# Softplus of the prompt attention by a capped exponent: the minimum on VectorE in place of the absolute value on ScalarE

## The chip, the cores and the metric

The kernel runs on one core of a Trainium2 chip. The metric is the device time in microseconds of one execution, the median of several; three runs of the kernel before gave 1794.58, 1794.62 and 1795.06.

## What is computed

One step of a hybrid decoder layer: a projection, stick-breaking attention and gated linear attention in parallel head groups, an output projection, an MLP and a final norm, for a prompt of 1024 tokens and for 8 sequences of 8 new tokens. What the change touches is the stick-breaking attention of the prompt (8 heads of 64, scores `z` with a bias, causal):

```python
log_stay = jnp.where(causal, jax.nn.log_sigmoid(-z), 0.0)
log_after = lax.cumsum(log_stay, axis=3, reverse=True) - log_stay
w = jnp.where(causal, jnp.exp(jax.nn.log_sigmoid(z) + log_after), 0.0)
return jnp.einsum("bhqk,bkhd->bqhd", w.astype(v.dtype), v)
```

Since log_sigmoid(-z) = -softplus(z) and log_sigmoid(z) = z - softplus(z), a weight is exp(z minus the sum of softplus over this key and all later ones). The kernel computes softplus, takes the sums off the scores by a matmul with a triangle of -1, and exponentiates.

## The kernel before

The stage is `stage_prompt_attention` (from line 1290). It stands between the sample attention and the gated linear attention and is closed by a barrier of all engines. Four pairs of heads are worked one after the other. A pair has twelve units, one for each block of 128 keys and chunk of 512 queries (`BLOCKS`): keys 7 down to 0 against the second chunk, then 3 down to 0 against the first. Blocks on the diagonal are narrower. With both heads together, the twelve units of a pair have 256, 512, 768 and five times 1024 columns, then 256, 512, 768 and 1024. This makes 48 units, called u below; `z(u, h)` is a unit's scores in two PSUM banks, out of a ring of three such slots (`NZ`).

Each engine has its own loop over steps s with a fixed order, and they meet by semaphores:

- TensorE (loop behind `subtract_later`, `carry`, `multiply`): scores of unit s (waits for the weights of s - 3, which frees the slot), the sums of unit s - 2 taken off its scores (waits for the low part of its softplus, and for the carry), the carry sum of s - 2, and the product with the values of unit s - 3.
- ScalarE: `absolute(s)`, `weights(s - 2)` (exponential out of PSUM, waits for the sums), `carry_hi(s - 2)`, then `exp_and_log(s)`, which is exp(-|z|) and log(1 + that), both within `pa_a`.
- VectorE: for the last unit of a chunk the two output instructions of unit s - 4 (`output`), then `softplus(s - 1)`: max(z, 0) + log (L1503, waits for the logarithm), the copy to the high part `pa_sh` (L1508), the low part `pa_sl` by subtraction (L1510); then `carry_lo(s - 2)` (L1518), which the next unit's sums wait for.
- SyncE loads queries and keys of a pair two pairs ahead, GpSimd scales the queries; both have nothing else to do here.

The lines which the argument names: L1464 absolute value, L1469 exponential, L1472 logarithm, L1478 weights, L1485 high carry (ScalarE); L1503, L1508, L1510, L1518, L1525 and L1527 (outputs) on VectorE; L1391 to L1400 scores, L1409 to L1415 sums, L1426 and L1428 carries, L1442 values on TensorE. L1918 lies in the stage behind.

Of the kernel before, what the change touches and what calls it, by code (L numbers as in the profile page):

```python
# [16 lines left out]
ALU = mybir.AluOpType  # L17
ACT = mybir.ActivationFunctionType
# [38 lines left out]
class Program:  # L57
# [22 lines left out]
    def sb(self, name, shape, dt=F32, ctx=None):  # L80
        return (ctx or self.ctx).enter_context(self.nc.sbuf_tensor(name, shape, dt))
# [27 lines left out]
def at_least(eng, sem, value):  # L109

    if not isinstance(value, int) or value > 0:
        eng.wait_ge(sem, value)
# [1177 lines left out]
def stage_prompt_attention(g, ops):  # L1290
# [9 lines left out]
    NPAIR = HEADS // 2  # L1300
    TOTAL = NPAIR * NB
    NZ, NA, NS, NW = 3, 3, 3, 3
    HALF = slice(0, HD), slice(HD, P)

    def block_of(u):
        c, j = BLOCKS[u % NB]
        return u // NB, c, j

    def left(c, j):
        return max(0, j - c * QB) * P  # L1310

    def width(u):
        p, c, j = block_of(u)
        return 512 - left(c, j)

    def halves(u):
        return [slice(0, 2)]

    def first(u):
        return u % NB in (0, 8)  # L1320

    def last(u):
        return u % NB in (7, 11)

    def carries_before(u):
        return NCARRY * (u // NB) + CARRY[u % NB]

    def multiplied(u):
        return u + 1

    with ExitStack() as ctx:
        sb = lambda *a: g.sb(*a, ctx=ctx)
        a_ = sb("pa_a", [P, NA, 2, 512])
# [2 lines left out]
        w = sb("pa_w", [P, NW, 2, 512])  # L1336
        later = ops.later
        s_z = g.sem("pa_scored")
        s_abs = g.sem("pa_abs")
        s_exp = g.sem("pa_exp")  # L1340
        s_ln = g.sem("pa_ln")
        s_sp = g.sem("pa_softplus")
        s_sh = g.sem("pa_softplus_hi")
        s_sl = g.sem("pa_softplus_lo")
# [12 lines left out]
        def z(u, h):  # L1357
            n = 2 * (u % NZ)
            return Z[:, n + h.start:n + h.stop, 0:width(u)]

        def ring(t, depth, u, h):
            return t[:, u % depth, h, 0:width(u)]

        with g.nc.Block() as block:
            @block.sync
            def _(sp):
                ops.load(sp, 0, 0)
                ops.load_values(sp)
                ops.load(sp, 1, 1)
                for p in range(2, NPAIR):  # L1370
                    sp.wait_ge(s_z, 2 * NB * (p - 1))
                    ops.load(sp, p, p % 2)
# [8 lines left out]
            def _(pe):  # L1381
                def score(u):
# [7 lines left out]
                    for h in range(2):  # L1390
                        pe.matmul(g.bank[2 * (u % NZ) + h][:, 0:n], ops.k[p % 2][HALF[h], keys], ops.q[p % 2][HALF[h], cols],  # L1391
                                  start=True, stop=False)
                    for h in range(2):
                        done = pe.matmul(g.bank[2 * (u % NZ) + h][:, 0:n], ops.bias[HALF[h], 2 * p + h, :], ops.ones[HALF[h], 0:n],
                                         start=False, stop=not diagonal)
# [36 lines left out]
                def multiply(u):  # L1432
# [7 lines left out]
                    for h in range(2):  # L1440
                        head = (2 * p + h) * HD
                        done = pe.matmul(O[HALF[h], x:512], ops.v[:, j, head:head + HD], w[:, u % NW, h, 0:n], start=first(u),  # L1442
                                         stop=last(u), skip_group_check=True)
# [12 lines left out]

            @block.scalar
            def _(act):
                def absolute(u):
                    for h in halves(u):  # L1460
                        n = 2 * u + h.stop
                        at_least(act, s_sl, n - 2 * NA)
                        act.wait_ge(s_z, n)
                        act.activation(ring(a_, NA, u, h), z(u, h), ACT.Abs).then_inc(s_abs, h.stop - h.start)  # L1464

                def exp_and_log(u):
                    for h in halves(u):
                        act.wait_ge(s_abs, 2 * u + h.stop)
                        act.activation(ring(a_, NA, u, h), ring(a_, NA, u, h), ACT.Exp, scale=-1.0).then_inc(s_exp, h.stop - h.start)  # L1469
                    for h in halves(u):  # L1470
                        act.wait_ge(s_exp, 2 * u + h.stop)
                        act.activation(ring(a_, NA, u, h), ring(a_, NA, u, h), ACT.Ln, bias=1.0).then_inc(s_ln, h.stop - h.start)  # L1472

                def weights(u):
                    at_least(act, s_pv, multiplied(u - NW))
                    for h in halves(u):
                        act.wait_ge(s_y, 2 * u + h.stop)
                        act.activation(ring(w, NW, u, h), z(u, h), ACT.Exp).then_inc(s_w, h.stop - h.start)  # L1478

                def carry_hi(u):  # L1480
                    if last(u):
                        return
                    m, x = carries_before(u), left(*block_of(u)[1:])
                    act.wait_ge(s_cs, m + 1)
                    act.copy(later[m % 2][:, x:512], C[:, x:512]).then_inc(s_eh, 1)  # L1485

                for s in range(TOTAL + 2):
                    if s < TOTAL:
                        absolute(s)
                    if s >= 2:  # L1490
                        weights(s - 2)
                        carry_hi(s - 2)
                    if s < TOTAL:
                        exp_and_log(s)

            @block.vector
            def _(dve):
                def softplus(u, h):
                    n = 2 * u + h.stop
                    inc = h.stop - h.start  # L1500
                    a = ring(a_, NA, u, h)
                    dve.wait_ge(s_ln, n)
                    dve.scalar_tensor_tensor(out=a, in0=z(u, h), scalar=0.0, in1=a, op0=ALU.max, op1=ALU.add).then_inc(s_sp, inc)  # L1503
                    dve.wait_ge(s_sp, n)
                    at_least(dve, s_y, n - 2 * NS)
                    if u >= NS:
                        dve.wait_ge(s_cs, carries_before(u - NS + 1))
                    dve.tensor_copy(ring(sh, NS, u, h), a).then_inc(s_sh, inc)  # L1508
                    dve.wait_ge(s_sh, n)
                    dve.tensor_tensor(ring(sl, NS, u, h), a, ring(sh, NS, u, h), ALU.subtract).then_inc(s_sl, inc)  # L1510

                def carry_lo(u):
                    if last(u):
                        return
                    m, x = carries_before(u), left(*block_of(u)[1:])
                    rows = HALF[1]
                    dve.wait_ge(s_eh, m + 1)
                    dve.tensor_tensor(later[m % 2][rows, x:512], C[rows, x:512], later[m % 2][rows, x:512],  # L1518
                                      ALU.subtract).then_inc(s_e, 1)

                def output(u):
                    p, c, j = block_of(u)
                    cols = slice(c * 512, (c + 1) * 512)
                    dve.wait_ge(s_pv, multiplied(u))
                    dve.tensor_copy(g.op_hi[:, p, cols], O).then_inc(s_oh, 1)  # L1525
                    dve.wait_ge(s_oh, 2 * p + 2 - c)
                    dve.tensor_tensor(g.op_lo[:, p, cols], O, g.op_hi[:, p, cols], ALU.subtract).then_inc(s_ol, 1)  # L1527

                ops.bias_rows(dve)
                samples = g.sample_o[:].rearrange("d p s q -> d p (s q)")  # L1530
                dve.tensor_copy(g.op_hi[:, 0:4, TP:T], samples).then_inc(s_so, 1)
                dve.wait_ge(s_so, 1)
                dve.tensor_tensor(g.op_lo[:, 0:4, TP:T], samples, g.op_hi[:, 0:4, TP:T], ALU.subtract).then_inc(s_so, 1)
                dve.wait_ge(s_so, 2)
                for s in range(TOTAL + 4):
                    if s >= 4 and last(s - 4):
                        output(s - 4)
                    parts = halves(s - 1) if 0 <= s - 1 < TOTAL else []
                    if parts:
                        softplus(s - 1, parts[0])  # L1540
                    if 0 <= s - 2 < TOTAL:
                        carry_lo(s - 2)
                    for h in parts[1:]:
                        softplus(s - 1, h)


def stage_gla(g):
# [9 lines left out]
    QS = GK ** -0.5  # L1557
    HALF = slice(0, GK), slice(GK, P)
    with ExitStack() as ctx:
# [103 lines left out]
        with nc.Block() as block:  # L1663
            @block.sync
            def _(sp):
# [29 lines left out]
                for h in range(2):  # L1695
                    for m in range(2):
                        sp.dma_start(s0[HALF[h], :, 2 * m + h, :], s0d[h, m]).then_inc(s_s0, 16)
                weights(6)
# [1123 lines left out]
```

## Time and profile before

| | before |
|---|---|
| median of 3 runs | 1794.62 us |
| profiled execution | 1795.72 us |
| its span | 1794.1 us |
| TensorE busy | 1657.8 us (92%) |
| VectorE busy | 724.1 us (40%) |
| ScalarE busy | 594.3 us (33%) |
| GpSimd busy | 432.5 us (24%) |

The profile is one execution. The page cuts its span into 40 equal slices of 44.9 us. A view by windows gives busy time in a stretch; the timeline has single instructions with start and length, and in brackets how long the engine stood idle ahead of one and what ended that. A busy engine is not one at its peak: matmuls overlap, and their ends are modelled.

### The profile page before, as it was taken

How to read it: one execution, taken by the hardware profiler on the slowest of the kernel's cores; microseconds unless marked ns; L12 is line 12 of the kernel's file. 1: busy time of each engine (PE TensorE's matmuls, PEld its weight loads, DVE VectorE, ACT ScalarE, POOL GpSimd, SP SyncE). 2: the span in 40 equal slices, each digit the busy share in tenths (PEclk: the TensorE clock that was granted, in tenths of full speed). 3: DMA queues.
4: the chain of work that ended last, by engine and by line, in shares of the span. 5: the costliest groups of instructions: out<-in, count | busy, mean ns of one | idle time of the engine just before them, and what ended most of it. 6: DMA issues, size and time to landing. Idle time of an engine off the chain costs nothing. (4 is left out here: it accounts for less than half of the span.)

```text
span 1794.1 us, 27592 instructions
## 1 busy us (share of the span) xinstructions
PE 1657.8 (92%) x10864; PEld 1449.6 (81%) x10864; DVE 724.1 (40%) x1157; ACT 594.3 (33%) x1010; POOL 432.5 (24%) x305
## 2 busy tenths in 40 slices
PE   5899997999979998587599899999999999999997
PEld 2898996777755554366499799999999999999997
DVE  2511021454457777478214733232323232323225
ACT  3521121333248887345235421202021212121123
POOL 0122112222200000201245542413242323323230
PEclk7899998999989999677699899999999999999999
DMA  9123126666420000853623211011111111111102
GB/s 335 48 98 106 53 100 205 222 186 220 136 107 24 24 1 1 274 176 123 220 94 110 79 48 42 29 47 47 47 47 47 47 47 30 40 46 47 47 12 100
DMA packets 116400, 166.62 MB, mean 93 GB/s; under 512 B 6970, under 2 KB 80141, under 8 KB 116054
## 3 DMA queue, kind: packets, MB, share of 16 engines
q1 hardware_dynamic: 111088, 148.58, 25.2%
q0 software_dynamic: 5120, 16.78, 2.9%
q8 instruction: 59, 0.97, 0.2%
q14 instruction: 31, 0.25, 0.0%
q10 hardware_dynamic: 102, 0.03, 0.0%
HBM read 143.03 MB, written 22.35 MB: 92 GB/s over the span
## 5 line engine op out<-in xcount | busy, mean ns | idle before, releaser
L469 PE MATMUL psum<-op_hi,out_hi 128*128 128x384 f32 (+1 forms) x960 | 320.9, 334 | 3.6 <-DVEq L2617 1.9
L471 PE MATMUL psum<-op_hi,out_lo 128*128 128x384 f32 (+1 forms) x960 | 314.6, 328 | 0.0
L470 PE MATMUL psum<-op_lo,out_hi 128*128 128x384 f32 (+1 forms) x960 | 314.5, 328 | 0.0
L469 PE MATMUL psum<-mlp_a_hi,out_hi 128*128 128x384 f32 (+1 forms) x768 | 251.0, 327 | 0.5 <-DVE x1T L2644 0.5
L471 PE MATMUL psum<-mlp_a_hi,out_lo 128*128 128x384 f32 (+1 forms) x768 | 250.8, 327 | 0.0
L470 PE MATMUL psum<-mlp_a_lo,out_hi 128*128 128x384 f32 (+1 forms) x768 | 250.5, 326 | 0.0
L2534 POOL TENSOR_TENSOR out_lo<-out_raw,out_hi 128x2048 fp32r<-128x2048 f32 x31 | 143.2, 4620 | 271.7 <-ACT out_hi L2557 271.7
L2630 DVE TENSOR_TENSOR mlp_sq<-mlp_relu 128x384 f32<-128x384 f32 (+1 forms) x96 | 88.3, 921 | 280.0 <-ACT mlp_relu L2572 280.0
L469 PEld LDWEIGHTS psum<-op_hi,out_hi 128*128 128x128 f32 x960 | 181.7, 189 | 7.8 <-DVEq L2617 2.8
L470 PEld LDWEIGHTS psum<-op_lo,out_hi 128*128 128x128 f32 x960 | 181.6, 189 | 2.5
L471 PEld LDWEIGHTS psum<-op_hi,out_lo 128*128 128x128 f32 x960 | 181.5, 189 | 0.0
L2644 DVE SCALAR_TENSOR_TENSOR x1T<-psum,modT,x1T 128x384 f32<-128x384 f32 (+1 forms) x192 | 108.6, 570 | 162.1 <-PE psum L471 155.1
L2557 ACT CAST out_hi<-out_raw 128x2048 fp32r<-128x2048 f32 x31 | 59.1, 1908 | 295.9 <-PE psum L471 295.9
L469 PEld LDWEIGHTS psum<-mlp_a_hi,out_hi 128*128 128x128 f32 x768 | 144.2, 188 | 0.8 <-POOL out_lo L2534 0.8
L471 PEld LDWEIGHTS psum<-mlp_a_hi,out_lo 128*128 128x128 f32 x768 | 144.2, 188 | 0.0
L470 PEld LDWEIGHTS psum<-mlp_a_lo,out_hi 128*128 128x128 f32 x768 | 144.1, 188 | 0.0
L2541 POOL TENSOR_TENSOR mlp_a_lo<-mlp_sq,mlp_a_hi 128x384 fp32r<-128x384 f32 (+1 forms) x96 | 92.7, 973 | 207.6 <-ACT mlp_a_hi L2564 207.6
L2572 ACT ACTIVATE mlp_relu<-psum 128x384 f32<-128x384 f32 (+1 forms) x96 | 45.5, 474 | 266.1 <-PE psum L471 266.1
L469 PE MATMUL psum<-op_hi,pg_hi 128*128 128x384 f32 (+1 forms) x192 | 76.4, 398 | 12.8 <-DVE pg_lo L1202 11.5
L590 POOL TENSOR_TENSOR in_lo<-in_raw,in_hi 128x2048 fp32r<-128x2048 f32 (+1 forms) x8 | 34.7, 4334 | 196.4 <-ACT in_hi L724 196.4
L469 PE MATMUL psum<-in_hi,op_hi 128*128 128x256 f32 (+1 forms) x288 | 81.4, 282 | 0.0
L471 PE MATMUL psum<-in_hi,op_lo 128*128 128x256 f32 (+1 forms) x288 | 80.4, 279 | 0.0
(339 smaller groups left out, 2988.5 us busy)
## 6 DMA issues: line engine op xcount, KB each, us to landing
sa_k<-in_cache_k SPq DMA_DIRECT2D x64, 256.0 KB, 3.0
sa_v<-in_cache_v POOLq DMA_DIRECT2D x64, 256.0 KB, 3.9
out_raw<-in_w_up SPq DMA_DIRECT2D x16, 1024.0 KB, 5.4
out_raw<-in_w_down SPq DMA_DIRECT2D x16, 1024.0 KB, 4.9
ada_w<-in_w_ada SPq DMA_DIRECT2D x26, 512.0 KB, 5.0
out_raw<-in_w_out SPq DMA_DIRECT2D x12, 1024.0 KB, 4.8
in_raw<-in_w_in SPq DMA_DIRECT2D x8, 1024.0 KB, 6.0
ada_w<-in_w_ada SPq DMA_DIRECT2D x3, 2048.0 KB, 13.7
```

The costliest lines, as they stand in the source:

```text
L469: pe.matmul(out, w_hi, x_hi, start=(k == 0), stop=False)
L470: pe.matmul(out, w_hi, x_lo, start=False, stop=False)
L471: return pe.matmul(out, w_lo, x_hi, start=False, stop=(k == nk - 1))
L590: pool.tensor_tensor(w.lo[p % 2][:, :, 0:n], w.raw[p % 2][:, :, 0:n], w.hi[p % 2][:, :, 0:n], ALU.subtract).then_inc(w.lo_done, 1)
L2534: pool.tensor_tensor(w.lo[s][:], w.raw[s][:], w.hi[s][:], ALU.subtract).then_inc(w.lo_done, 1)
L2541: pool.tensor_tensor(a_lo[:, m, t0:t0 + tw], q[i % 3][:, 0:tw], a_hi[:, m, t0:t0 + tw], ALU.subtract).then_inc(s_al, 1)
L2557: act.copy(w.hi[s][:], w.raw[s][:]).then_inc(w.hi_done, 1)
L2572: act.activation(r[i % 3][:, 0:tw], g.bank[i % NBANK][:, 0:tw], ACT.Relu).then_inc(s_re, 1)
L2630: dve.tensor_tensor(q[i % 3][:, 0:tw], r[i % 3][:, 0:tw], r[i % 3][:, 0:tw], ALU.mult).then_inc(s_sq, 1)
L2644: dve.scalar_tensor_tensor(out=out, in0=b[:, 0:pw], scalar=g.mod(GA2, kc), in1=out, op0=ALU.mult, op1=ALU.add).then_inc(s_dn, 1)
```

## The change

The absolute value on ScalarE goes, with its wait for a free buffer and for the scores. VectorE writes min(z, 30) from PSUM into `pa_a` instead, in a loop step of its own ahead of `softplus(s - 1)`. ScalarE takes exp of that (without the scale of -1) and log(1 + ...), as before in place. The instruction at L1503 is now max(z x 1.0, log) in place of max(z, 0) + log. Where z is over 30, log(1 + exp(30)) is smaller than z and the maximum gives z.

```diff
+    CAP = 30.0
...
-        s_abs = g.sem("pa_abs")
+        s_cap = g.sem("pa_capped")
...
             def _(act):
-                def absolute(u):
-                    for h in halves(u):
-                        n = 2 * u + h.stop
-                        at_least(act, s_sl, n - 2 * NA)
-                        act.wait_ge(s_z, n)
-                        act.activation(ring(a_, NA, u, h), z(u, h), ACT.Abs).then_inc(s_abs, h.stop - h.start)
-
                 def exp_and_log(u):
                     for h in halves(u):
-                        act.wait_ge(s_abs, 2 * u + h.stop)
-                        act.activation(ring(a_, NA, u, h), ring(a_, NA, u, h), ACT.Exp, scale=-1.0).then_inc(s_exp, h.stop - h.start)
+                        act.wait_ge(s_cap, 2 * u + h.stop)
+                        act.activation(ring(a_, NA, u, h), ring(a_, NA, u, h), ACT.Exp).then_inc(s_exp, h.stop - h.start)
...
                 for s in range(TOTAL + 2):
-                    if s < TOTAL:
-                        absolute(s)
...
-                    dve.scalar_tensor_tensor(out=a, in0=z(u, h), scalar=0.0, in1=a, op0=ALU.max, op1=ALU.add).then_inc(s_sp, inc)
+                    dve.scalar_tensor_tensor(out=a, in0=z(u, h), scalar=1.0, in1=a, op0=ALU.mult, op1=ALU.max).then_inc(s_sp, inc)
...
+                def capped(u):
+
+                    for h in halves(u):
+                        n = 2 * u + h.stop
+                        at_least(dve, s_sl, n - 2 * NA)
+                        dve.wait_ge(s_z, n)
+                        dve.tensor_scalar(ring(a_, NA, u, h), z(u, h), CAP, None, ALU.min).then_inc(s_cap, h.stop - h.start)
...
                 for s in range(TOTAL + 4):
                     if s >= 4 and last(s - 4):
                         output(s - 4)
+                    if s < TOTAL:
+                        capped(s)
                     parts = halves(s - 1) if 0 <= s - 1 < TOTAL else []
```

## Rows read from the trace of the kernel before

**Rows 1.** The page, granted TensorE clock in 40 slices, in tenths.

```profile
PEclk7899998999989999677699899999999999999999
```

**Rows 2.** Windows: length, busy PE, PEld, DVE, ACT, POOL, clock, DMA share, GB/s.

```profile
518.00:722.00 204.00, 185.31 (x976) 102.04 (x976) 152.23 (x200) 163.16 (x232) 4.80 (x5) 0.99 0.07 26
586.60:591.41 4.81, 4.81 (x23) 2.49 (x21) 3.83 (x5) 4.64 (x6) 0.00 (x0) 1.00 0.01 3
```

**Rows 3.** The waits, 518 to 722 us: total us, times, longest.

```profile
DVE pa_a L1503 <- ACT pa_a L1472: 35.2, 33, 4.0
```

**Rows 4.** Groups of instructions by form: count, busy us, mean ns, idle before.

```profile
L1464 ACT ACTIVATE pa_a<-psum 128x1024 f32<-128x1024 f32 x24 | 24.4, 1015 | 3.5 <-PE psum L1400 3.5
L1918 DVE TENSOR_SCALAR gl_pt<-psum 128x512 f32<-128x512 f32 x8 | 5.5, 691 | 3.4 <-PE psum L2024 3.2
```

**Rows 5.** The timeline of VectorE, 647 to 662 us: start, length, instruction.

```profile
647.31 1.23 DVE L1503 SCALAR_TENSOR_TENSOR pa_a<-psum,pa_a 128x1024 f32<-128x1024 f32 x1 [0.83 <-ACT pa_a L1472]
648.63 0.69 DVE L1508 CAST pa_sh<-pa_a 128x1024 fp32r<-128x1024 f32 x1
649.43 1.22 DVE L1510 TENSOR_TENSOR pa_sl<-pa_a,pa_sh 128x1024 fp32r<-128x1024 f32 x1
650.68 0.69 DVE L1518 TENSOR_TENSOR pa_later<-psum,pa_later 64x512 fp32r<-64x512 f32 x1
651.41 0.42 DVE L1503 SCALAR_TENSOR_TENSOR pa_a<-psum,pa_a 128x256 f32<-128x256 f32 x1
651.92 0.29 DVE L1508 CAST pa_sh<-pa_a 128x256 fp32r<-128x256 f32 x1
652.32 0.43 DVE L1510 TENSOR_TENSOR pa_sl<-pa_a,pa_sh 128x256 fp32r<-128x256 f32 x1
655.11 0.69 DVE L1503 SCALAR_TENSOR_TENSOR pa_a<-psum,pa_a 128x512 f32<-128x512 f32 x1 [2.37 <-ACT pa_a L1472]
655.89 0.43 DVE L1508 CAST pa_sh<-pa_a 128x512 fp32r<-128x512 f32 x1
656.43 0.69 DVE L1510 TENSOR_TENSOR pa_sl<-pa_a,pa_sh 128x512 fp32r<-128x512 f32 x1
657.15 0.29 DVE L1518 TENSOR_TENSOR pa_later<-psum,pa_later 64x128 fp32r<-64x128 f32 x1
657.47 0.69 DVE L1525 CAST op_hi<-psum 128x512 fp32r<-128x512 f32 x1
658.20 0.69 DVE L1527 TENSOR_TENSOR op_lo<-psum,op_hi 128x512 fp32r<-128x512 f32 x1
658.81 0.95 DVE L1503 SCALAR_TENSOR_TENSOR pa_a<-psum,pa_a 128x768 f32<-128x768 f32 x1
659.84 0.56 DVE L1508 CAST pa_sh<-pa_a 128x768 fp32r<-128x768 f32 x1
660.51 0.96 DVE L1510 TENSOR_TENSOR pa_sl<-pa_a,pa_sh 128x768 fp32r<-128x768 f32 x1
661.50 0.43 DVE L1518 TENSOR_TENSOR pa_later<-psum,pa_later 64x256 fp32r<-64x256 f32 x1
```

**Rows 6.** The timeline of ScalarE in the same stretch.

```profile
655.25 0.81 ACT L1464 ACTIVATE pa_a<-psum 128x768 f32<-128x768 f32 x1 [0.24 <-PE psum L1400]
```

**Rows 7.** The timeline at the start and at the end of the stage.

```profile
520.12 0.38 ACT L1464 ACTIVATE pa_a<-psum 128x256 f32<-128x256 f32 x1 [13.38 <-PE psum L1400]
521.81 0.60 ACT L1464 ACTIVATE pa_a<-psum 128x512 f32<-128x512 f32 x1 [0.28 <-PE psum L1400]
...
529.08 0.96 DVE L1510 TENSOR_TENSOR pa_sl<-pa_a,pa_sh 128x768 fp32r<-128x768 f32 x1
...
713.50 1.23 DVE L1510 TENSOR_TENSOR pa_sl<-pa_a,pa_sh 128x1024 fp32r<-128x1024 f32 x1
```

**Rows 8.** Windows of 12 us, in this stage and the next; columns as in rows 2.

```profile
562.00:574.00 12.00, 9.58 (x60) 5.59 (x59) 8.33 (x12) 8.43 (x15) 1.04 (x1) 1.00 0.18 71
778.00:790.00 12.00, 9.85 (x81) 7.00 (x79) 7.97 (x18) 6.62 (x20) 1.27 (x1) 0.78 0.61 196
```

## The prediction

> **What bounds the kernel now.** I read the page's forty slices first, then the waits, then the timeline of single steps. The change touches only prompt attention, which runs from 518 to 722 us, from slice 12 of the page into slice 17. The granted clock reads nine tenths or more in slices 13 to 16 [rows 1] and 0.99 in the mean of the stage [rows 2], which is its upper level, 2.4 GHz, nearly throughout. In that stretch TensorE is busy 185.31 us of 204.00, ScalarE 163.16 and VectorE 152.23 [rows 2]. So TensorE has the least to spare, but that is a mean over two kinds of step. The stage has 48 units in four rounds of twelve. One round has six wide units (128x1024 for both heads together) and two each of 768, 512 and 256 columns. In a wide step TensorE is busy 4.81 us of 4.81, ScalarE 4.64 and VectorE 3.83 [rows 2]: TensorE sets the pace and both others wait. Around the narrow units all three wait for one another in turn. VectorE waited 35.2 us in all for ScalarE's logarithm [rows 3], and in the timeline it stands still for 2.37 us ahead of the 512-wide unit [rows 5].
>
> What I need from VectorE is not the length of each row but the distance from one start to the next, because that has the gap between instructions in it. One stretch of the timeline shows all shapes in turn [rows 5]. The softplus chain of one unit (maximum, copy to high part, subtraction) takes 650.68 - 647.31 = 3.37 us for 1024 columns, 661.50 - 658.81 = 2.69 for 768, 657.15 - 655.11 = 2.04 for 512, and for 256 columns 652.32 - 651.41 and 0.46 for its last, 1.37. A carry takes 0.73 us at 512 columns and 0.32 at 128, 0.46 at 256 (0.43 and a gap of 0.03), and I set 0.59 for 384, halfway between its neighbours. The two output instructions take 658.81 - 657.47 = 1.34 us. One round of VectorE is then 6 x 3.37 + 2 x (2.69 + 2.04 + 1.37) = 32.42 for the chains, 4 x 0.73 + 2 x (0.32 + 0.46 + 0.59) = 5.66 for ten carries and 2 x 1.34 = 2.68 for outputs, together 40.8 us. The rounds take (714.73 - 520.12) / 4 = 48.7 us each, from the first absolute value to the end of the last subtraction [rows 7]. VectorE has about 8 us to spare per round.
>
> **The change part by part.**
>
> *ScalarE loses the absolute value.* 48 instructions go, the wide one at 1015 ns [rows 4]. In wide steps TensorE has no idle time to give back, so this earns nothing there. Before the narrow units ScalarE waits for scores and for sums, so it has time anyway. I cost the removal at nothing. The exponential keeps its form, with another scale. What covers the loss of a gain is TensorE's 4.81 us; if ScalarE and not TensorE were the pace, up to 0.9 us a step would be earned, which is the third rival.
>
> *VectorE gains the minimum.* The trace of before has no minimum from PSUM at this size. The nearest row is the TENSOR_SCALAR from PSUM of 128x512 in the stage behind this one, mean 691 ns [rows 4], the same as 0.69 us of the two-operand maximum at 512 columns [rows 5]. I take from this that one more operand makes no difference when the source lies in PSUM, and give the minimum the length of the maximum, 1.23 us at 1024 columns [rows 5], which is 1.25 us from start to start with a gap of 0.03. At 768, 512 and 256 columns the distances of the subtraction stand for it, 0.99, 0.72 and 0.46 us [rows 5]. A round then has 6 x 1.25 + 2 x (0.99 + 0.72 + 0.46) = 11.8 us more, and four rounds 47.4 us. The bounds of this price are the copy of 1024 columns within SBUF, 0.69 us [rows 5], and the maximum with its gap of 0.09, 1.32 us [rows 5]. I stay at the upper row, since it reads PSUM and the copy doesn't.
>
> The Trainium skill says in "VectorE: DVE Perf Modes", section "Rules for kernel authors", that elementwise work on a matmul's output either accepts the plain rate or is copied to SBUF first; in "ScalarE: Activation LUTs", section "Rules for kernel authors", it says to use VectorE, not ScalarE, for a minimum or maximum. By the second rule the move is a gain; by the first it has the plain rate, and 691 ns for 512 columns from PSUM agrees with that [rows 4].
>
> *The rest of VectorE's work.* The maximum is still one two-operand instruction with a source in PSUM, so its price stays. Bounds of a change there are zero on both sides.
>
> *The order.* The minimum of unit s is queued on VectorE ahead of the whole softplus chain of unit s - 1, and behind it stand that chain and the carry of s - 2. It waits for the score of s. The score waits for a PSUM slot, that is for the weights of unit s - 3, and these for the subtraction of s - 3. So each minimum starts no earlier than the end of subtraction s - 3 plus the way through TensorE and ScalarE. For a wide step this way is one TensorE step, 4.81 us, and up to 0.3 for the carry which the sums also wait for, together 5.1. VectorE has 0.73 + 1.25 + 3.37 + 0.73 = 6.1 us of its own work in between, so there is no stall. A wide step costs VectorE 1.25 + 3.37 + 0.73 = 5.35 us against TensorE's 4.81. VectorE becomes the pace, and TensorE waits 0.5 us a step.
>
> Two times a round it does stall. The subtraction of the last unit of a block row ends at 649.43 + 1.22 = 650.65 [rows 5], and ScalarE can read the score of the third unit behind it at 655.25 [rows 6], 4.6 us later. VectorE's own work in between is a carry, the minimum of 512 and the chain of 256: 0.73 + 0.72 + 1.37 = 2.8 us in one case and 0.59 + 0.72 + 1.37 = 2.7 in the other. The stalls are 1.8 and 1.9 us. They are the old stalls of 2.4 us, filled by the minimum of one unit only.
>
> **The sum.** A round becomes 40.8 + 11.8 + 1.8 + 1.9 = 56.3 us. For the first round I go through the start. The first minimum starts where the absolute value did, 520.12. The second waits for its score until 521.81 [rows 7] and the first chain waits behind it: 521.81 + 0.72 + 1.37 = 523.9. Then 0.99 + 2.04 + 0.32 + 1.25 + 2.69 brings the third subtraction to 531.2, against 529.08 + 0.96 = 530.04 before [rows 7]. The five chains up to the eighth unit are 0.46 + 4.62 + 0.59 + 4.62 + 0.73 + 4.62 + 0.73 + 4.62 + 0.73 + 0.46 + 3.37 = 25.5, which gives 556.7. The four units behind it take 4.6 + 0.99 + 2.04 + 0.32 + 1.34 + 1.25 + 2.69 + 0.46 + 0.46 + 3.37 = 17.5, which gives 574.2. Three rounds of 56.3 bring 743.1, less 0.46 for the minimum of a unit that isn't there, 742.6. Before, the last subtraction ended at 713.50 + 1.23 = 714.73 [rows 7]. What comes behind is the same chain as before, and a barrier closes the stage, so the difference goes through whole: 742.6 - 714.7 = 27.9 us, rounded down to 27.5 because handovers of 4.6 us may be some tenths shorter. The profiled execution took 1795.72 us with a span of 1794.1, which stands 1.1 us above the median 1794.62. On the median I forecast 1794.6 + 27.5 = 1822 us. If all stalls of VectorE vanished, the stage would still be 4 x 52.6 - 1.8 (no last output and minimum) - 194.6 = 14 us longer. If the minimum overlapped with no wait at all it would be 47 us.
>
> **The rivals.**
>
> *The minimum runs at the SBUF copy's rate.* Then it takes 0.72 us from start to start at 1024 columns, and by the copy's rows 0.59, 0.46 and 0.32 at the others, a round 7.1 instead of 11.8 us. The stalls grow by 0.26 each, since less work fills them. A round is 56.3 - 4.8 + 0.5 = 52.0 us, a wide step 4.82, level with TensorE. From 27.5 us the 3.75 rounds from the first wide step on take 16 back: +11 us, 1806. The minimum has one tensor operand, like the copy, which speaks for it; the 691 ns row, also with one, against. The table of rates in the Trainium skill ("VectorE: DVE Perf Modes", section "The perf-mode tier table (the rule you actually need)") leaves such an instruction up to twice the plain rate from any PSUM; the same row of 691 ns speaks against that. Chance 0.08.
>
> *TensorE's clock falls.* TensorE would be busy 46 of 56 us, 82%. In the next stage a stretch with 9.85 us busy of 12 has a mean granted clock of 0.78, and in this stage one with 9.58 of 12 has 1.00 [rows 8]. If the stage went at 0.78, TensorE's 185.3 us would become 238 and with its 18.7 us of idle time 256 against 204, +52: 1847. TensorE keeps working in every step and its longest pauses become shorter or stay, which speaks against. Chance 0.07.
>
> *The minimum hides, and ScalarE's relief counts.* Place: the narrow steps, where weights are queued behind an absolute value. If ScalarE is what holds TensorE there, and VectorE's waits swallow the minimum, part of TensorE's idle time could come back. It idles 2.4 us in the stretch from 562 to 574 [rows 8], some 10 in four rounds; half of that is 5 us: 1790, faster. The rule quoted above from "ScalarE: Activation LUTs" in the Trainium skill would have it end on this side. It decides where a round of VectorE with stalls falls below 48.7, that is where the minimum's round costs less than 48.7 - 40.8 - 3.7 = 4.2 us, 0.45 us per wide minimum. Nothing in the rows is so short from PSUM. Chance 0.04: 0.02 for it and 0.02 for a balance that leaves no change.
>
> **How the numbers follow.** The forecast has 0.81; its own range is 1814 to 1829, from the price of the minimum (1.22 to 1.32 us) and handovers of 4.0 to 5.4 us. To reach 8 in 10 the range is 1806 to 1834, which takes in the cheap minimum and a little of a falling clock. About 0.2% (3.6 us) is what a measurement of this kernel can tell from no change. Slower by more: 0.96. Within: 0.02. Faster: 0.02.
>
> **What the profile after would show.** The minimum as 48 TENSOR_SCALAR rows on VectorE at about 1225 ns for 128x1024; VectorE some 198 us busy in the stage (152.2 and 24 x 1.23 + 8 x (0.95 + 0.69 + 0.42)); wide steps 5.35 us apart on all engines, with VectorE's wait for the logarithm gone; ScalarE some 125 us busy, waiting mostly for the minimum; two stalls of nearly 2 us a round ahead of the minimum of 768 columns; the stage some 27 us longer and all behind it only moved. A wide minimum of 0.7 us, or a clock below 1.00 in the stage, would make it wrong.

## The result and the profile after

| | before | after |
|---|---|---|
| median | 1794.84 us (4 runs) | 1821.49 us (4 runs, 1817.82 to 1823.81) |
| ratio, 95% interval | | 1.0141, 1.0128 to 1.0153 |
| profiled execution, span | 1795.72, 1794.1 | 1817.82, 1816.1 |
| stage, first score to the memset behind its barrier | 518.79 to 720.97, 202.2 us | 516.7 to 746.1, 229.4 us |
| attention stage behind it, to its first store of the state | 140.4 us | 137.2 us |

The change costs 26.7 us in the medians; 27.5 were forecast. The interval of the ratio lies wholly above 1. The profiled execution of after is the quickest of its four. It is 22.1 us over that of before: 2.1 us less ahead of the stage, 27.2 more in it, 3.2 less in the stage behind it, nothing in the rest.

The granted clock by slices (page of after), and the stage as windows (columns as in rows 2), the whole first, then six microseconds of it:

```profile
PEclk9999998999989999777699899999999999999999
```

```profile
516.70:746.10 229.40, 196.53 (x976) 109.07 (x976) 195.14 (x248) 131.86 (x184) 3.15 (x4) 0.94 0.06 22
...
680.00:686.00 6.00, 6.00 (x26) 4.26 (x26) 4.18 (x6) 2.02 (x4) 0.00 (x0) 0.62 0.01 3
```

VectorE is now busy 195.1 of 229.4 us where it was 152.2 of 204.0 [rows 2], and ScalarE 131.9 where it was 163.2. TensorE reads 196.5 instead of 185.3 with the same 976 matmuls: the granted clock is 0.94 in the mean and not 0.99, so some of them took longer. How often the clock fell, and what it cost, stands below under the clock.

The groups of the minimum and of its neighbours in the stage, and the waits (columns as in rows 3 and 4):

```profile
L1510 DVE TENSOR_SCALAR pa_a<-psum 128x1024 f32<-128x1024 f32 x24 | 29.3, 1222 | 0.5
L1495 DVE SCALAR_TENSOR_TENSOR pa_a<-psum,pa_a 128x1024 f32<-128x1024 f32 x24 | 29.4, 1225 | 0.7
L1510 DVE TENSOR_SCALAR pa_a<-psum 128x768 f32<-128x768 f32 x8 | 7.7, 957 | 12.2 <-PE psum L1401 12.2
...
ACT pa_w L1472 <- PE psum L1416: 72.4, 40, 2.6
PE psum L1410 <- DVE pa_sl L1502: 26.7, 23, 3.3
DVE pa_a L1510 <- PE psum L1401: 18.1, 12, 2.6
```

The minimum takes 1222 ns at 1024 columns, as long as the two-operand maximum (1225). VectorE's old wait, 35.2 us for the logarithm [rows 3], is gone from the list; what is left are 18.1 us ahead of the minimum, 12.2 of them ahead of the eight with 768 columns. TensorE waits 26.7 us for VectorE where it waited 10.5. That is a row of the waits of before which the groups above don't have:

```profile
PE psum L1409 <- DVE pa_sl L1510: 10.5, 12, 1.9
```

VectorE's timeline: one wide step, the stall ahead of the 768-wide minimum, the start of one round's first output and of the next one's, and the two ends of the loop:

```profile
534.53 1.23 DVE L1510 TENSOR_SCALAR pa_a<-psum 128x1024 f32<-128x1024 f32 x1
535.79 1.22 DVE L1495 SCALAR_TENSOR_TENSOR pa_a<-psum,pa_a 128x1024 f32<-128x1024 f32 x1
537.10 0.69 DVE L1500 CAST pa_sh<-pa_a 128x1024 fp32r<-128x1024 f32 x1
537.90 1.23 DVE L1502 TENSOR_TENSOR pa_sl<-pa_a,pa_sh 128x1024 fp32r<-128x1024 f32 x1
539.16 0.69 DVE L1518 TENSOR_TENSOR pa_later<-psum,pa_later 64x512 fp32r<-64x512 f32 x1
539.88 1.23 DVE L1510 TENSOR_SCALAR pa_a<-psum 128x1024 f32<-128x1024 f32 x1
...
559.01 0.96 DVE L1510 TENSOR_SCALAR pa_a<-psum 128x768 f32<-128x768 f32 x1 [1.82 <-PE psum L1401]
...
562.24 0.69 DVE L1525 CAST op_hi<-psum 128x512 fp32r<-128x512 f32 x1
...
572.65 0.69 DVE L1510 TENSOR_SCALAR pa_a<-psum 128x512 f32<-128x512 f32 x1 [0.40 <-PE psum L1401]
...
618.22 0.69 DVE L1525 CAST op_hi<-psum 128x512 fp32r<-128x512 f32 x1
...
518.12 0.42 DVE L1510 TENSOR_SCALAR pa_a<-psum 128x256 f32<-128x256 f32 x1 [2.58 <-PE psum L1401]
...
738.52 1.23 DVE L1502 TENSOR_TENSOR pa_sl<-pa_a,pa_sh 128x1024 fp32r<-128x1024 f32 x1
```

From minimum to minimum a wide step is 539.88 - 534.53 = 5.35 us, and no row in it has idle time in front. A round from output to output is 618.22 - 562.24 = 55.98 us.

### The profile page after: what moved, and what is told of

Same layout as the page of the kernel before. It is cut to its first block and busy times, and to the rows that moved or that the text cites. A ratio compares the mean times of both kernels' runs of the same rounds, so it can differ in the third digit from the quotient of the medians.

```text
span 1816.1 us, 27592 instructions
## 1 busy us (share of the span) xinstructions
PE 1663.8 (92%) x10864; PEld 1453.0 (80%) x10864; DVE 767.3 (42%) x1205; ACT 562.8 (31%) x962; POOL 432.6 (24%) x305
```

## Experiments

Each is timed against the kernel before on the same chip. A round is taken as above, from the first output copy of one pair to that of the next. Of the kernel before these starts are 558.99, 608.35, 657.47 and 706.22, so 49.4, 49.1 and 48.8 us.

| kernel | median, us | ratio, 95% interval | rounds, us |
|---|---|---|---|
| after, again | 1821.22 | 1.0137, 1.0115 to 1.0158 | 55.5, 56.0, 55.6 |
| copy on ScalarE | 1795.36 | 1.0001, 0.9991 to 1.0010 | 49.4, 50.3, 48.7 |
| before and an extra VectorE instruction | 1823.63 | 1.0156, 1.0139 to 1.0172 | 56.3, 57.0, 55.9 |
| two minimums | 1860.59 | 1.0357, 1.0340 to 1.0374 | 65.4, 67.4, 65.6 |
| minimum behind the chain | 1866.02 | 1.0390, 1.0372 to 1.0407 | 66.5, 66.2, 66.5 |
| cap in the maximum | 1794.67 | 0.9991, 0.9980 to 1.0003 | 49.1, 48.9, 48.2 |
| the same, exponential first | 1783.77 | 0.9932, 0.9916 to 0.9949 | 46.8, 46.8, 46.0 |
| minimum on half the columns | 1801.90 | 1.0027, 1.0016 to 1.0038 | 51.5, 51.2, 51.2 |

### The changed kernel again

> The changed kernel once more, for its spread: its runs lay between 1817.8 and 1823.8. Theory (the stage is the same each time and what varies is TensorE's granted clock outside VectorE's reach): the stage takes 229 us again, the total 1818 to 1824, and a difference to the first profile lies in the stages around. Rival (a clock that falls within the stage lengthens it): the stage itself differs by over 2 us.

The stage took 228.9 us (518.1 to 747.0) against 229.4, and the stage behind it 141.9 us against 137.2. The spread lies there: the two executions differ by 4.7 us in that stretch, in which nothing is changed. The second execution's window of it:

```profile
747.00:888.90 141.90, 106.55 (x734) 77.32 (x734) 94.48 (x195) 61.68 (x181) 18.37 (x24) 0.71 0.58 182
```

In the quicker execution the same stretch has the same 734 matmuls at a clock of 0.73. So the 22.1 us between the profiled executions understate the change, and the medians with 26.7 agree with the stage's 27. The first profile was no unusual one in the stage itself.

### Is it the formula or the place of the work?

The heart of the edit against the changed kernel; the waits around the instruction move with it:

```diff
-                        dve.tensor_scalar(ring(a_, NA, u, h), z(u, h), CAP, None, ALU.min).then_inc(s_cap, h.stop - h.start)
...
+                        act.activation(ring(a_, NA, u, h), z(u, h), ACT.Identity).then_inc(s_cap, h.stop - h.start)
```

The copy stands in ScalarE's loop where the absolute value stood.

> The changed kernel, but ScalarE writes a plain copy of z where the minimum wrote its capped one (the cap is left out, so exp takes z as it is); the new maximum and the new exponential stay. Theory (the loss is the minimum's time on VectorE): as before the change, stage 202 us, 1795 us, ratio 1.000 within 0.002. Rival (the new formula costs something of its own, in the exponential of large arguments or in the maximum with a product): over 1800.

No difference to the kernel before can be measured. The new maximum, the exponential without the negative scale and the larger range of its arguments together cost nothing beyond 0.1% (the interval is 0.9991 to 1.0010); the loss comes with the minimum on VectorE.

### VectorE's time alone

Against the kernel before; the buffers, the first filling of `pa_fill` and the place of the call, which is that of the minimum, are left out here:

```diff
...
+                        dve.wait_ge(s_z, n)
+                        dve.tensor_tensor(ring(spare, NA, u, h), fill[:, h, 0:width(u)], fill[:, h, 0:width(u)], ALU.add).then_inc(s_x, h.stop - h.start)
...
```

> The kernel before, with its absolute value on ScalarE, and one more VectorE instruction a unit at the place of the minimum, of the same length (two-operand add within SBUF, 1225 ns at 1024 columns), which also waits for the scores and for whose result nobody waits. Theory (VectorE's time alone is the loss, ScalarE's relief is worth nothing): +27 us in the stage, 1821. Rival A (ScalarE's relief gave part of the loss back): clearly more, 1826 or above. Rival B (the exponential's wait for the minimum is a good part of the loss): clearly less, 1815 or below.

1823.6 us, within 2.2 of the changed kernel and with overlapping intervals, although ScalarE still computes its absolute value and no other engine waits for the added instruction. So the exponential's wait for the minimum is not what costs the time. From the second round on its outputs are 38.5 us apart over the wide part, as in after. The stage took 232.8 us, 3.4 more than after. 1.9 of these lie ahead of the first output, and there the clock differs. The windows at the start of this kernel:

```profile
517.90:524.00 6.10, 6.08 (x29) 3.74 (x29) 3.09 (x6) 3.88 (x7) 0.00 (x0) 0.50 1.05 404
524.00:530.00 6.00, 6.00 (x25) 4.07 (x25) 4.17 (x7) 3.85 (x6) 1.37 (x1) 0.50 0.08 33
```

and of after:

```profile
516.70:523.00 6.30, 5.84 (x34) 3.80 (x34) 3.44 (x7) 2.54 (x6) 0.00 (x0) 0.68 1.02 398
523.00:529.00 6.00, 4.88 (x29) 2.70 (x30) 5.46 (x9) 4.66 (x7) 1.05 (x1) 1.00 0.09 33
```

TensorE ran the first 12 us of the stage at 1.2 GHz here, and in after only part of the first 6 (0.68). Over the whole stage the clock is 0.91 here and 0.94 in after. The other 1.5 us fall in narrow parts; whether they are the clock too or the absolute value's share of ScalarE's time isn't settled. They are the most that ScalarE's relief can have given back.

### Twice the price

Against the changed kernel, without the lines of the spare buffer:

```diff
+                        dve.tensor_scalar(ring(spare, NA, u, h), z(u, h), CAP, None, ALU.min).then_inc(s_x, h.stop - h.start)
                         dve.tensor_scalar(ring(a_, NA, u, h), z(u, h), CAP, None, ALU.min).then_inc(s_cap, h.stop - h.start)
```

> The changed kernel with the minimum done twice, first into a spare buffer. Theory (VectorE is the pace, stalls fill a little): a wide step of 5.35 + 1.25 = 6.60 us; a round 40.8 + 23.7 + 1.1 + 1.2 = 66.8 us against 56.3; 40 us more than the changed kernel, 1861. Rival (waits and handovers hold the loop, the minimum is partly hidden): 20 us more or less, 1841.

1860.6 against 1861 expected; the rival had 1841. A wide step of its timeline:

```profile
606.72 1.22 DVE L1513 TENSOR_SCALAR pa_spare<-psum 128x1024 f32<-128x1024 f32 x1
607.87 1.21 DVE L1514 TENSOR_SCALAR pa_a<-psum 128x1024 f32<-128x1024 f32 x1
...
613.21 1.23 DVE L1513 TENSOR_SCALAR pa_spare<-psum 128x1024 f32<-128x1024 f32 x1
```

It takes 6.49 us, 1.14 more and not 1.25: two minimums in a row from the same scores overlap by 0.07 us, so the second one starts 1.15 behind the first. VectorE pays nearly the full price of what is added, and the wide steps aren't held by waits. The stage's clock was lower too, 0.89 in the mean of 516 to 786 us; what that added isn't separated.

### The place in VectorE's queue

```diff
-                    if s < TOTAL:
-                        capped(s)
                     parts = halves(s - 1) if 0 <= s - 1 < TOTAL else []
                     if parts:
                         softplus(s - 1, parts[0])
+                    if s < TOTAL:
+                        capped(s)
```

> The changed kernel with the minimum of unit s queued behind the softplus chain of unit s - 1 instead of ahead of it. Same instructions. Theory (place matters: the logarithm of unit s then takes minimum, exponential and logarithm in a row just ahead of its chain): stalls of 1.6 us in a wide step, so 6.95 us each, a round 52.6 + 14 = 66.6 us, 1862 in all. Rival (only the sum of VectorE's work counts): 1821.

1866.0 against 1862 expected, a round 66.2 to 66.5 against 66.6. The same instructions cost 45 us more when the minimum stands behind the chain. The reading on which this was expected is that the exponential and the logarithm of the unit then have only the carry to hide behind. The wide steps of the timeline and VectorE's longest entry among the waits agree:

```profile
606.02 0.56 DVE L1518 TENSOR_TENSOR pa_later<-psum,pa_later 64x384 fp32r<-64x384 f32 x1
608.40 1.22 DVE L1495 SCALAR_TENSOR_TENSOR pa_a<-psum,pa_a 128x1024 f32<-128x1024 f32 x1 [1.81 <-ACT pa_a L1466]
...
615.27 1.23 DVE L1495 SCALAR_TENSOR_TENSOR pa_a<-psum,pa_a 128x1024 f32<-128x1024 f32 x1 [1.68 <-ACT pa_a L1466]
...
DVE pa_a L1495 <- ACT pa_a L1466: 63.4, 48, 1.9
```

A step is 615.27 - 608.40 = 6.87 us with 1.7 to 1.8 idle. VectorE waited for the logarithm ahead of all 48 chains, 63.4 us in all.

### Neither the minimum nor the absolute value

Against the changed kernel; `capped` and its call are gone too, and the exponential has its two waits:

```diff
-                        act.activation(ring(a_, NA, u, h), ring(a_, NA, u, h), ACT.Exp).then_inc(s_exp, h.stop - h.start)
+                        act.activation(ring(a_, NA, u, h), z(u, h), ACT.Exp).then_inc(s_exp, h.stop - h.start)
...
-                    dve.scalar_tensor_tensor(out=a, in0=z(u, h), scalar=1.0, in1=a, op0=ALU.mult, op1=ALU.max).then_inc(s_sp, inc)
+                    dve.scalar_tensor_tensor(out=a, in0=a, scalar=CAP, in1=z(u, h), op0=ALU.min, op1=ALU.max).then_inc(s_sp, inc)
```

The maximum has room for the cap: max(min(log(1 + exp z), 30), z) is z wherever the log is too large, so the exponential may take z as it stands. What the exponential and the logarithm give for scores far above 30 no run looks at.

> No minimum and no absolute value: ScalarE takes exp(z) straight from PSUM, then log(1 + that), and VectorE's one instruction is max(min(log, 30), z). The cap is kept, behind the logarithm. Theory (wide steps stay at TensorE's 4.8 us, the stalls at the narrow units get shorter by the absolute value, 0.6 to 0.8 us each, up to 3 us a round): 1784 to 1793. Rival (TensorE and VectorE hold the loop everywhere, ScalarE's relief is worth nothing): 1795.

The rival was right and my theory wrong: 1794.7, no gain that can be told from none. 48 instructions are gone from ScalarE, its busy time in the stage falls from 163.2 to 128.6 us, and nothing comes of it. In the order of this kernel the exponential stands behind the weights, and these wait for the sums.

> As the kernel with the cap in the maximum, but ScalarE's order is exponential of s, weights of s - 2, high carry of s - 2, logarithm of s; there the absolute value stood before. Theory: the exponential no longer stands behind the weights and uses the wait for the sums, 0 to 3 us less than the other order. Rival: the weights come later by the exponential and TensorE's scores with them, some us more.

This order, exponential ahead of the weights, brings 1783.8 us, ratio 0.9932, and the stage takes 191.9 us (516.3 to 708.2) instead of 202.2. My theory expected 3 us at most from the order, and it was 11 (1794.7 to 1783.8); against the kernel before it is 12 us on the same chip. The waits of the stage in the kernel with the exponential behind the weights, and then in this one:

```profile
ACT pa_w L1473 <- PE psum L1415: 56.1, 40, 4.0
DVE pa_a L1496 <- ACT pa_a L1467: 33.1, 30, 3.6
ACT pa_a L1464 <- PE psum L1400: 14.2, 2, 13.4
```

```profile
ACT pa_a L1464 <- PE psum L1400: 39.4, 29, 13.3
ACT pa_w L1475 <- PE psum L1415: 26.3, 28, 3.0
DVE pa_a L1500 <- ACT pa_a L1469: 19.3, 16, 3.5
```

ScalarE's idle time ahead of the weights falls from 56 to 26 us, since the exponential runs in it; most of that idle time has moved to a place ahead of the exponential, where ScalarE now waits 39.4 us for scores instead of 14.2. And VectorE gets its logarithms earlier: it waits 19.3 us instead of 33.1. Of the wide steps the middle ones stay at TensorE's pace (585.48 to 590.29, 4.81 us from score to score); the gain, 2.3 to 2.8 us a round against the kernel before, lies in the narrow units and in the wide ones next to them. This version beats both kernels.

### Half the minimum

VectorE's part of the edit against the changed kernel:

```diff
-                        dve.tensor_scalar(ring(a_, NA, u, h), z(u, h), CAP, None, ALU.min).then_inc(s_cap, h.stop - h.start)
+                        dve.tensor_scalar(ring(a_, NA, u, slice(0, 1)), z(u, slice(0, 1)), CAP, None, ALU.min).then_inc(s_cap, 1)
...
```

ScalarE's part is an exponential for each head instead of one for both; that of the second head comes first and doesn't wait for VectorE. So this run shortens the minimum and also loosens half of the wait for it.

> The changed kernel with the minimum on the first head only, half the columns; the second head's exponential reads its scores straight from PSUM (the cap is left out there), so ScalarE has two exponentials of half the width. Theory (the loss is VectorE's time with the stalls, down to the point where TensorE takes over the pace): a minimum of 0.72 us from start to start in a wide step, wide steps of 3.37 + 0.73 + 0.72 = 4.82 us, level with TensorE's 4.81; a round 40.8 + 7.1 + 4.2 of stalls = 52.1 us against 48.7 before and 56.3 after; +11 us over the kernel before, 1806. Rival A (half the minimum, half the loss): +13 or 14, 1809. Rival B (so short a minimum hides in VectorE's waits): 1796 to 1799.

Wide steps came out at 4.81 us, the stalls at 2.04 and 2.05:

```profile
590.84 0.69 DVE L1513 TENSOR_SCALAR pa_a<-psum 128x512 f32<-128x512 f32 x1
...
595.65 0.69 DVE L1513 TENSOR_SCALAR pa_a<-psum 128x512 f32<-128x512 f32 x1
...
608.72 0.56 DVE L1513 TENSOR_SCALAR pa_a<-psum 128x384 f32<-128x384 f32 x1 [2.04 <-PE psum L1401]
```

The steps are as expected and the stage is 9.7 us longer than before (517.9 to 729.8), near the 11 expected. The total is only 5.1 us up in the medians of that chip, less than the theory and Rival A and more than Rival B's upper end of 1799. The two figures can be brought together. The profiled execution, 1803.28, is 7.6 us over that of the kernel before: 9.7 more in the stage, 0.9 less ahead of it, 1.2 less behind it. It lies 1.4 above its own median, and the kernel before's median on that chip, 1796.8, lies 1.1 above 1795.72; 7.6 - 1.4 - 1.1 = 5.1. A stage read from one execution isn't sharp to the microsecond either: the copy kernel, with the time of the kernel before, had a stage of 204.5 us.

By the stage or by the total, a minimum at 0.72 / 1.25, or six tenths, of the price costs 36% or 19% of the loss. So the loss isn't proportional. That it begins where VectorE's round passes that of the others fits this, but the looser wait in the same edit isn't ruled out as part of it.

## Why the prediction was right

**Who sets the pace.** The reading that wide steps belong to TensorE and that VectorE would take them over held to the hundredth: 4.81 before, 5.35 after, in the middle wide steps of a round. With the cap in the maximum and the exponential first, they are at 4.81 with ScalarE relieved of a microsecond a step, so it was TensorE and not ScalarE.

**The price of the minimum.** 1.23 us was taken from the maximum, 1222 ns was measured, in 24 rows. The choice of the upper bound, by where the source lies, was the right one; the lower bound would have given 1806. A pair of the rows of before bears the reason out, and the prediction didn't use it: the same copy of 512 columns takes 0.43 us out of SBUF (L1508) and 0.69 us out of PSUM (L1525) [rows 5].

In the Trainium skill it is "VectorE: DVE Perf Modes", section "Why PSUM operands drop a tier", that says an operand in PSUM leaves the plain rate for fp32; 1222 ns for one tensor operand and 1225 for two agree with it. The table of rates in the section "The perf-mode tier table (the rule you actually need)" allows up to twice the plain rate from PSUM, which no fp32 row here shows. The advice in "ScalarE: Activation LUTs", section "Rules for kernel authors", to use VectorE for a minimum, gives a rate for bf16 as its reason. Here, with fp32 out of PSUM, the time went up by 1.4%.

**The order and the stalls.** No stall in wide steps: none seen. Two stalls a round, 1.8 and 1.9 us: 1.82 and 1.77 in the timeline. Not forecast were 0.40, 0.20 and 1.56 us ahead of three of the 512-wide minimums. All three lie in parts of a round in which the clock fell; where it didn't (563.90 to 580.92 in the second execution) that minimum has no idle time in front.

**The sum.** From the first minimum to the end of the last subtraction 739.75 - 518.12 = 221.6 us, forecast 742.6 - 520.12 = 222.5, before 194.6. So +27.0 for +27.9. A round was forecast at 56.3 and measured at 55.5 to 56.8. That the sum is so close is in part luck, since two errors had opposite signs. The part with the narrow units has distances shorter than the prediction's: 0.61 us instead of 0.72 from an output to the minimum, 1.13 instead of 1.25 from that minimum to the maximum behind it. From the second execution:

```profile
564.63 0.69 DVE L1527 TENSOR_TENSOR op_lo<-psum,op_hi 128x512 fp32r<-128x512 f32 x1
565.24 1.22 DVE L1510 TENSOR_SCALAR pa_a<-psum 128x1024 f32<-128x1024 f32 x1
566.37 0.95 DVE L1495 SCALAR_TENSOR_TENSOR pa_a<-psum,pa_a 128x768 f32<-128x768 f32 x1
```

Its first round, whose narrow part had the full clock, took 55.5 us, 0.8 less than forecast. The falls of the clock, put at nothing, made other rounds longer. One number in the prediction was loose: 48.7 us for a round of before was the loop's length through four, which leaves out the start and the end; from output to output it is 49.1.

**ScalarE's relief at nothing.** Right, and for the reason given only in part. I named TensorE's pace as what hides it. That holds for wide steps. Around the narrow ones it is also the order on ScalarE: without a minimum, and with the exponential behind the weights, the relief is worth nothing that can be measured (1794.7); with the exponential in the place of the absolute value the kernel is 11 us faster (1783.8). The third rival had priced it at 5 us and had asked for a cheaper minimum, not for another order.

**Busy times.** I had added 46 us to VectorE's 152.2 and expected 198; the stage shows 195.1. The rows of copies got shorter (24 of 1024 columns: 16.7 us, before 17.6), and rows that overlap are counted once. ScalarE has 131.9 where I expected 125, for the same reason: its absolute values had overlapped their neighbours.

**The clock, where the prediction was wrong.** I wrote that TensorE's longest pauses would become shorter or stay, and that a clock below 1.00 in the stage would make the forecast wrong. Both failed, though the time came out. The mean clock fell from 0.99 to 0.94. TensorE's pauses ahead of the sums grew from 1.9 to 3.3 us at most, by the waits. Seven of them last 1.98 us or more, and at six of the seven the clock fell to 1.2 GHz for a stretch, within the pause or up to about a microsecond behind it. In the second execution pauses of the same lengths had four falls. One pause, on TensorE, with what followed on VectorE:

```profile
679.19 0.69 PE L1410 MATMUL psum<-pa_sh,pa_negtri 128*128 128x384 f32 x1 [2.57 <-DVE pa_sl L1502]
683.52 1.22 PE L1392 MATMUL psum<-pa_q,pa_k 64*128 64x256 f32 x4
...
685.57 0.69 DVE L1510 TENSOR_SCALAR pa_a<-psum 128x512 f32<-128x512 f32 x1 [1.56 <-PE psum L1401]
```

The scores of 256 columns took 1.22 us instead of 0.70, and the minimum behind them waited 1.56 us. The windows between outputs (columns as in rows 2) give the cost. First the three parts with the narrow units and two of those with the wide ones, in after, then two parts with narrow units in the second execution:

```profile
562.24:579.71 17.47, 14.30 (x84) 8.66 (x84) 14.27 (x22) 9.48 (x15) 1.05 (x1) 0.90 0.17 61
618.22:635.49 17.27, 14.10 (x84) 9.12 (x84) 14.27 (x22) 9.48 (x15) 1.04 (x1) 0.90 0.18 62
674.01:692.27 18.26, 15.10 (x84) 9.56 (x84) 14.26 (x21) 9.48 (x15) 0.00 (x0) 0.81 0.01 1
579.71:618.22 38.51, 34.70 (x164) 18.37 (x164) 34.52 (x41) 23.54 (x31) 0.00 (x0) 0.96 0.00 1
635.49:674.01 38.52, 33.42 (x164) 17.35 (x164) 34.52 (x41) 23.42 (x31) 0.00 (x0) 1.00 0.00 0
...
563.90:580.92 17.02, 13.12 (x84) 7.75 (x84) 14.27 (x21) 9.37 (x15) 1.05 (x1) 1.00 0.18 63
675.42:692.51 17.09, 13.91 (x84) 9.10 (x84) 14.26 (x21) 9.48 (x15) 0.00 (x0) 0.90 0.01 1
```

With the wide units a fall cost nothing: at 0.96 TensorE is busy 1.3 us longer than at 1.00 and the part is as long. With the narrow ones the part at the full clock took 17.02 us, those with a fall 0.1 to 0.5 more, and the one at 0.81 took 1.2 more. In after this adds up to some 2 us of the stage's 27 (an estimate: the last round has no part at the full clock to compare with). So the step that failed is the second rival's condition, put aside with the argument that the pauses wouldn't grow. Its price of 52 us was wrong by far, because it took the low clock for the whole of the stage and TensorE for the pace, while the falls were short and a TensorE behind VectorE has time to be slow in.

## What to carry to other kernels

Before moving work to an engine with idle time, add up its round in start-to-start distances and compare with the pace of the loop: here 8 us of slack a round met 12 us of work plus 4 of stalls that can't be filled. Taking work away can earn nothing until the order on that engine lets the next step use the time: the same 48 instructions less brought nothing measurable, or 12 us, by where the exponential stood. And look first whether an instruction that is there already has a free operand for the step: with the cap inside it the maximum still took 1221 ns, and the kernel had the time of the one before.

## What the runs showed of the hardware

- Where one VectorE instruction doesn't need the result of the one ahead of it, it can start before that one ends: 1.15 us behind a minimum of 1024 columns with a length of 1.22 (two minimums), 1.13 us behind one at the start of a round (565.24 to 566.37). In the wide steps of after the distance behind the minimum is 1.26. What decides between the two isn't shown.
- The granted clock fell to 1.2 GHz in stretches of the stage (0.62 in the mean of 680 to 686 us in after), during or soon behind pauses of TensorE of 1.98, 2.57 and 3.27 us, but not at all of these pauses: at six of seven in one execution, at four of seven in the other. Neither is 1.98 us a limit: with the copy on ScalarE the clock fell behind a pause of 1.40 us (0.81 in the mean of 611 to 617 us), while pauses of 1.28 and 1.59 us in the kernel before had no fall.
- The same 734 matmuls of the stage behind took 137.2 us in one execution and 141.9 in another of the same kernel, at 0.73 and 0.71 of full clock: here is most of the 5.7 us between the two.
